# Low-rank products one pair ahead and row work regrouped in the RWKV-7 stage of a decoder step

## The reference

```python
wlog = -softplus(-(w0 + tanh(xw @ w1) @ w2)) - 0.5
decay = exp(-exp(wlog))
a = sigmoid(a0 + (xa @ a1) @ a2)
g = sigmoid(xg @ g1) @ g2
kk = heads(k * p_kk); kk = kk / max(norm(kk), 1e-12)
k = k * (1 + (a - 1) * ka)
S, y = wkv7_scan(S0, r, decay, k, v, -kk, kk * a)
yn = (y - mean(y)) * rsqrt(var(y) + eps) * lnw + lnb
bonus = sum(r * k * rk, -1) * v
out = ((yn + bonus) * g) @ wo
```

## Time and profile before

| what | value |
|---|---|
| three runs | 2943.74, 2944.91 (median), 2949.14 us |
| profiled execution, its own time | 2936.58 us |
| its span | 2934.8 us |
| TensorE, share of the span | 91% |
| VectorE, ScalarE, GpSimd | 56%, 46%, 15% |
| pair stage, from the first key norm sums to the last finish | about 1352 to 1965 us |
| mean granted TensorE clock | 0.963 |

### The profile page before, as it was taken

One profiled execution on the slowest core, in us unless ns is written; L12 is line 12 of the kernel. 1 busy time (PEld: TensorE's weight loads), 2 busy tenths in 40 slices (PEclk: granted clock), 3 DMA queues, 4 the chain that ended last, 5 costly groups with the idle time before them and its releaser, 6 DMA issues.

```text
span 2934.8 us, 69044 instructions
## 1 busy us (share of the span) xinstructions
PE 2683.1 (91%) x25416; PEld 2580.2 (88%) x25416; DVE 1642.7 (56%) x2457; ACT 1352.4 (46%) x2301; POOL 428.3 (15%) x806
## 2 busy tenths in 40 slices
PE   3899999999999699997887778779899999999997
PEld 2799999999999699997666666669899999999997
DVE  7665545654564777335555555634656546654654
ACT  1577435553453455333443444433577435543552
POOL 3221001110112200000111111112112001100112
PEclk7899999999999899999999999989999999999999
DMA  3444444444444444441000000024455444444444
GB/s 114 156 162 152 165 158 157 150 164 157 157 152 144 152 146 168 156 163 69 14 25 25 25 25 25 25 85 165 140 161 168 168 160 163 164 165 165 164 144 142
DMA packets 113726, 378.37 MB, mean 129 GB/s; under 512 B 12080, under 2 KB 22960, under 8 KB 113328
## 3 DMA queue, kind: packets, MB, share of 16 engines
q1 hardware_dynamic: 113584, 376.26, 38.2%
HBM read 363.61 MB, written 12.60 MB: 128 GB/s over the span
## 4 chain that ended last, share of the span: by engine, by line
PE 87%; DVE 7%; ACT 3%; issue 3%; POOL 0%; DMA 0%; DVEq 0%; ACTq 0%; POOLq 0%
PE bank L542 24%; PE bank L544 24%; PE bank L543 24%; PE bank L654 11%; PE bank L620 1%; DVE ysd L1289 1%; DVE pext L1358 1%; ACT L1012 1%; DVE tb L1266 1%; PE bank L794 0%; PE bank L853 0%; DVE ar L1296 0%; PE bank L797 0%; PE bank L604 0%; DVE rnorm L1148 0%
## 5 line engine op out<-in xcount | busy, mean ns | idle before, releaser
L1141 DVE TENSOR_TENSOR wlo<-raw,whi 128x1024 fp32r<-128x1024 f32 (+1 forms) x672 | 794.5, 1197 | 776.7 <-ACT whi L875 775.8
L542 PE MATMUL bank<-h_hi,whi 128*128 128x290 f32 (+1 forms) x3520 | 1059.3, 301 | 45.2 <-DVE h_lo L1167 38.1
L875 ACT ACTIVATE whi<-raw 128x1024 fp32r<-128x1024 f32 (+1 forms) x672 | 685.3, 1032 | 836.5 <-PE bank L544 815.2
L544 PE MATMUL bank<-h_hi,wlo 128*128 128x290 f32 (+1 forms) x3520 | 1056.8, 300 | 0.0
L543 PE MATMUL bank<-h_lo,whi 128*128 128x290 f32 (+1 forms) x3520 | 1056.0, 300 | 0.0
L542 PEld LDWEIGHTS bank<-h_hi,whi 128*128 128x128 f32 x3520 | 668.2, 190 | 49.7 <-issue 44.2
L543 PEld LDWEIGHTS bank<-h_lo,whi 128*128 128x128 f32 x3520 | 668.7, 190 | 0.0
L544 PEld LDWEIGHTS bank<-h_hi,wlo 128*128 128x128 f32 x3520 | 668.5, 190 | 0.0
L542 PE MATMUL bank<-act_hi,whi 128*128 128x304 f32 (+1 forms) x1376 | 410.1, 298 | 1.1 <-DVE act_lo L1226 1.1
L544 PE MATMUL bank<-act_hi,wlo 128*128 128x304 f32 (+1 forms) x1376 | 410.4, 298 | 0.0
L543 PE MATMUL bank<-act_lo,whi 128*128 128x304 f32 (+1 forms) x1376 | 409.7, 298 | 0.0
(11 more groups left out here) (209 smaller groups left out, 3024.9 us busy)
## 6 DMA issues: line engine op xcount, KB each, us to landing
raw<-W_all SPq DMA_DIRECT2D x648, 512.0 KB, 3.3
raw<-W_all SPq DMA_DIRECT2D x32, 192.0 KB, 3.1
wkv_out<-sout SPq DMA_DIRECT2D x16, 288.0 KB, 2.2
l<-L_all SPq DMA_DIRECT2D x16, 256.0 KB, 2.8
s<-wkv_st SPq DMA_DIRECT2D x16, 256.0 KB, 3.0
x<-xT SPq DMA_DIRECT2D x4, 608.0 KB, 6.1
x_spill<-x SPq DMA_DIRECT2D x1, 2432.0 KB, 7.2
x<-x_spill SPq DMA_DIRECT2D x1, 2432.0 KB, 9.4
```

The lines of the kernel that those rows point to most:

```text
L542: mm_(acc, wh, xh, start=first, stop=False)
L544: return mm_(acc, wl, xh, start=False, stop=last)
L875: activation(WHI[q][:, 0:n], RAW[q][:, 0:n], ACT.Copy).then_inc(whi_ready, 1)
L1141: tt(WLO[q][:, 0:n], RAW[q][:, 0:n], WHI[q][:, 0:n].bitcast(f32), ALU.subtract).then_inc(wlo_ready, 1)
```

## The change

The decay's and a's low-rank products of pair n+1 are made in the joint of iteration t, behind the bonus sums, beside the gate products of pair n, which move there from the joint's end. They write to banks 6, 7 and 1. ScalarE's tanh, exp, tanh and KP for pair n+1 follow in the joint, then the gate copy. The mean sums wait for KP (`kp_ready`), since they use bank 7, and the final state products for the gate copy. A new first iteration t = -2 makes the two products for pair 0. ScalarE's `affine` goes from step 0 to step 3, VectorE's `k_rows` from step 4 to step 3. SP loads L2 before it waits for the output state. The copy of y waits for `at_ready` in place of `out_ready` where there is an inverse.

```diff
@@ pipeline
+        iteration(FIRST_STAGE, 0, operands=False, inverse=False, chain=False, finish=False)
         iteration(-1, 1, inverse=False, chain=False, finish=False)
@@ SP, pair_io
-                sp.wait_ge(fin_ready, p)
-                sp.dma_start(wkv_out[p - 1].rearrange("p (b n) -> p b n", b=9), SOUT).then_inc(wkv_stored, 16)
                 if weights:
                     sp.wait_ge(gg_ready, p + 1)
                     sp.dma_start(L2[i], L2_all[p + 2]).then_inc(l2_loaded[i], 16)
+                sp.wait_ge(fin_ready, p)
+                sp.dma_start(wkv_out[p - 1].rearrange("p (b n) -> p b n", b=9), SOUT).then_inc(wkv_stored, 16)
@@ TensorE, steps
                     if operands and s_ == 0:
-                        if later(n):
-                            pe.wait_ge(gg_ready, n)
+                        if chain and later(j):
+                            pe.wait_ge(var_ready, j)
+                        elif not chain:
+                            pe.wait_ge(kp_ready, n + 1)
                         pe.wait_ge(kksq_ready, n + 1)
...
-                    if operands and s_ == 1:
-                        pe.wait_ge(kkroot, n + 1)
-                        pe.wait_ge(l2_loaded[m], by_parity(n, m))
-                        mm_(bank[7][:, 0:TOK], L2[m][:, 0:128], hidden[:, 0, :], start=True, stop=True).then_inc(z_mm, 1)
-                    if operands and s_ == 2:
-                        pe.wait_ge(gates_ready, n + 1)
-                        mm_(bank[7][:, 0:TOK], L2[m][:, 128:256], hidden[:, 1, :], start=True, stop=True).then_inc(lora_mm, 1)
@@ TensorE, joint, behind the bonus sums
+                if gates:
+                    pe.wait_ge(l2_loaded[par], by_parity(n + 1, par))
+                    if operands:
+                        pe.wait_ge(kkroot, n + 1)
+                    wide(bank[6], L2[par], 0, 0).then_inc(z_mm, 1)
+                    wide(bank[7], L2[par], 128, 1).then_inc(lora_mm, 1)
+                if operands:
+                    wide(bank[1], L2[m], 256, 2, stop=False)
+                    wide(bank[1], L2[m], 384, 3, start=False).then_inc(gate_mm, 1)
                 if chain:
-                    pe.wait_ge(*((kp_ready, n + 1) if operands else (gg_ready, PAIRS)))
+                    if gates:
+                        pe.wait_ge(kp_ready, n + 2)
                     pe.wait_ge(y_ready, j + 1)
...
+                    if operands:
+                        pe.wait_ge(gg_ready, n + 1)
                     pe.wait_ge(sax_ready, j + 1)
...
+                    if gates:
+                        pe.wait_ge(gates_ready, n + 2)
                     waited()
                     turned(bank[5], BR)
                     turned(bank[6], KR).then_inc(trans_bk_mm, 1)
-                    pe.wait_ge(*((var_ready, j + 1) if chain else (kp_ready, n + 1)))
-                    mm_(bank[7][:, 0:TOK], L2[m][:, 256:384], hidden[:, 2, :], start=True, stop=False)
-                    mm_(bank[7][:, 0:TOK], L2[m][:, 384:512], hidden[:, 3, :], start=False, stop=True).then_inc(gate_mm, 1)
@@ ScalarE
-                    if finish and s_ == 0:
+                    if finish and s_ == 3:
                         act.wait_ge(scaled, t - 1)
                         activation(YY[par_], YY[par_], ACT.Identity, scale=par("lnw", t - 2), bias=par("lnb", t - 2)).then_inc(affine, 1)
...
-                        if finish:
-                            act.wait_ge(out_ready, t - 1)
+                        act.wait_ge(*((at_ready, t + 1) if inverse else (out_ready, t - 2)))
                         act.wait_ge(y_mm, j + 1)
                         activation(YY[m], bank[0][:, 0:TOK], ACT.Copy).then_inc(y_ready, 1)
+                if gates:
+                    act.wait_ge(z_mm, n + 2)
+                    steps.done(activation(DEC[:, 0:TOK], bank[6][:, 0:TOK], ACT.Tanh, bias=w0_half[:, ds(n + 1)], scale=0.5))
+                    steps.wait()
+                    activation(DEC[:, 0:TOK], DEC[:, 0:TOK], ACT.Exp, scale=0.5 * DECAY_SCALE, bias=decay_bias)\
+                        .then_inc(gates_ready, 1)
+                    act.wait_ge(lora_mm, n + 2)
+                    if operands:
+                        act.wait_ge(rkk_ready, n + 1)
+                    steps.done(activation(TA[:, 0:TOK], bank[7][:, 0:TOK], ACT.Tanh, bias=a0_half[:, ds(n + 1)], scale=0.5))
+                    steps.wait()
+                    activation(KP[:, 0:TOK], TA[:, 0:TOK], ACT.Identity, scale=ka_half[:, ds(n + 1)], bias=ka_rest[:, ds(n + 1)])\
+                        .then_inc(kp_ready, 1)
                 if operands:
+                    act.wait_ge(gate_mm, n + 1)
+                    act.sem_inc(act_gate, 1)
+                    activation(k_all[:, n, :], bank[1][:, 0:TOK], ACT.Copy).then_inc(gg_ready, 1)
                     act.wait_ge(x2_mm, n + 1)
@@ VectorE
-                steps_n = {1: norms, 2: decays, 3: b_rows, 4: k_rows}
+                def rows():
+                    b_rows()
+                    k_rows()
+
+                steps_n = {1: norms, 2: decays, 3: rows}
```

More of the change, by code:

```diff
@@ L303, in build @@
         y_mm s_mm sp_ready s_ready y_ready sax_ready vx_ready fin_mm fin_ready mean_mm centered ycsq_ready gram_b_mm
-        sout_ready stk_ready trans_bk_mm var_mm var_ready gnroot scaled affine out_ready wkv_stored tile_gate pool_gate""".split()
+        sout_ready stk_ready trans_bk_mm var_mm var_ready gnroot scaled affine out_ready wkv_stored tile_gate pool_gate act_gate""".split()
     (lora_mm, gate_mm, kksum_mm, bonus_mm, trans_mm, gram_mm, gates_ready, kp_ready, kksq_ready, kkroot,
@@ L309, in build @@
      sout_ready, stk_ready, trans_bk_mm, var_mm, var_ready, gnroot, scaled, affine, out_ready, wkv_stored,
-     tile_gate, pool_gate) = [sem(n) for n in RSEMS]
+     tile_gate, pool_gate, act_gate) = [sem(n) for n in RSEMS]
     xset_ready = [sem(f"xset_ready{z}") for z in range(2)]
     s0_loaded = [sem(f"s0_loaded{i}") for i in range(2)]
+    FIRST_STAGE = -2
     LV = 5
@@ L668, in iteration @@
                 n, m, j = t + 1, 1 - par, t - 1
+                gates = not isinstance(t, int) or t + 2 < PAIRS
                 def t1_products(l, z):
@@ L821, in iteration @@
                     head_sums(bank[5], TB).then_inc(bonus_mm, 1)
+                wide = lambda dst, l2, at, i, start=True, stop=True: mm_(dst[:, 0:TOK], l2[:, at:at + 128], hidden[:, i, :],
+                                                                       start=start, stop=stop)
+                if gates:
[7 more added lines that the diff above has]
+                    wide(bank[1], L2[m], 384, 3, start=False).then_inc(gate_mm, 1)
                 if chain:
-                    pe.wait_ge(*((kp_ready, n + 1) if operands else (gg_ready, PAIRS)))
+                    if gates:
+                        pe.wait_ge(kp_ready, n + 2)
                     pe.wait_ge(y_ready, j + 1)
@@ L1038, in iteration @@
                 if operands:
-                    act.wait_ge(gate_mm, n + 1)
                     act.wait_ge(trans_bk_mm, n + 1)
@@ L1043, in iteration @@
                     ins.then_inc(tok_act, 1)
-                    activation(k_all[:, n, :], bank[7][:, 0:TOK], ACT.Copy).then_inc(gg_ready, 1)
             decay_bias = 0.5 * DECAY_SCALE
```

## The result

The changed kernel takes 2973.73 us (median of 4 runs, 2973.1 to 2975.51) against 2944.32 us of the kernel before on the same chips (4 runs). The ratio is 1.0098, interval 1.0084 to 1.0112: 1% slower. The sign was forecast, the size was not: +29 us against +6, outside the range of 2932 to 2962.

A forecast was written before the change was run, and what follows sets the result against it. TensorE was taken as the bound, busy 80% at mean clock 0.92 in the loop. Full-clock pairs +2.4, clock +2.0 and ends +1.8 made +6.2 us on 2944.9: 2951.1, range 2932 to 2962.

The forecast's parts named there:

- The joint: Stretch from Gram products to the pair's end: two added products and the mean's wait for ScalarE, +2.1 us a pair.
- The tanh table load is hidden: In the joint: ScalarE stands idle during the Gram products, so the load adds nothing to the mean's wait.
- rival E: In the joint: the tanh load isn't hidden, 13 x 1.28 = +16.6 us, giving 2967.7; chance 0.06.
- The affine's place: Moved from step 0 to step 3: step 0 to 1 gains 1.3 us, AR comes 1.2 later.
- The wait for KP: In the joint, before the mean sums: TensorE idles 0.7 to 0.8 us until ScalarE's KP.
- the steps: Steps 0 to 3, update to update: gains of 1.3, 1.3 and 0.5 us a pair, VectorE's T1 coming last.
- Step 0 to 1: With affine moved, RHS is early and T1 comes last: gain 1.3 us a pair.
- GpSimd's two operations: Step 3 to the joint: they hold up VectorE's tb and AR products, Gram products 1.2 us later; bounds 0 to 1.65.
- moving the rows: Step 3 to the joint: key and bonus rows change places with T1 of step 4, cost 0.
- the back edge: At the loop's end: TensorE's wait keeps its 2.7 us, bounds -1 to +1 in each of five.
- The clock: Half clock in all twelve joints, +8.3 us; less half clock in step 1, -6.3; together +2.0.
- The ends: Before and after the loop: start and first pairs +6.8 us, last iterations and chain -5.0, together +1.8.

The follow-up runs named there:

- e1: The changed kernel with a one-element tanh on ScalarE behind the copy of y, ahead of the wait for the z product: 2947.8 us.
- e3: The changed kernel with the decay tanh's bias taken from one fixed column instead of the loop's: 2944.84 us, one run.
- e2: The changed kernel with ScalarE's affine at the end of step 1 instead of step 3: 2949.59 us.
- e8: The kernel before with only the key rows and the bonus product moved into step 3: 2931.78 us.
- e7: The changed kernel with an early tanh load, the affine at the end of step 1 and the mean sums ahead of the z product: 2917.65 us.
- e4: The kernel before with only ScalarE's affine moved from step 0 to step 3: 2953.36 us.

## Why the prediction was wrong

**The step that failed** is the one in "The joint" that says "The tanh table load is hidden: ScalarE stands idle there during the Gram products, and the sqrt load of the same joint ran before its wait". It was reasoned from a load whose activation has no operand indexed by the loop. That was rival E, put at 0.06 and priced at 1.28 us a pair. e1 and e3 show it, at 26 us with what the clock added; E's own price was 16.6. Without that term the time lies in the range: with the load early the kernel takes 2947.8, 3 us from the forecast 2951.1. The affine's place costs nearly as much (24 us, e2), but that stood in the sum, as 1.2 us a pair and 8.3 by the clock. The wait for KP, forecast at 0.7 to 0.8, is then 0.9.

**Right within the working:** the steps. Clean distances of the kernel after are 4.62 and 4.28 us from update to update (4.6 and 4.4 forecast), and T1 became the last to come. Step 0 to 1: 6.62 to update 1, 6.8 forecast. The steps' gain is 3.6 us a pair, forecast 3.1 and 0.5 by the clock.

**GpSimd's two operations:** Gram products 0.8 us later than before, 1.2 forecast. The two moves inside that number were mixed: the affine in step 3 costs 1.2 (after against e2), and moving the rows gains 0.4 (before against e8), which I had put at 0. So the stall was sized rightly and the rows' own gain was missed: with the rows first, part of SAX falls beside T1 of step 4, and in e8 the first AR product is stretched by 0.6 us where `tb` had lost 0.94.

**The joint** was forecast at +2.1. It came to 4.3 a pair: 2.1, the load's 1.3, 0.6 by half clock behind the longer wait, and the back edge. Its wait, one in every second pair, was 2.4 to 2.8 us and is now 3.2 to 3.6, where I had kept 2.7 with bounds of 1: 0.3 a pair.

**The clock.** All twelve joints now begin at half clock, as forecast: 4.05 us from Gram products to bonus sums against 2.96, 1.1 a pair where I had 0.7 (five more slow joints). The slow ones also became slower, with 4.29 in seven of them, so that the Gram products ran at half clock throughout. In the steps the prediction counted seven pairs with half clock in step 1; the trace of before has five of them (6.7 to 6.9 us from update 1 to 2), worth 4.2 us and not 6.3.

**The ends.** The stage begins its loop 5.0 us later (1435.8 against 1430.8), 6.8 forecast. From the last operands' pair to the last finish 82.9 us against 84.5: 1.6 gained, 5.0 forecast; the joint of that pair too starts at half clock (4.29 us to the bonus sums instead of 2.20), which I had counted at the clean pair's length.

**Together:** 5.0 + 32.1 - 1.6 = 35.5 of the 36.5 us between the two profiled spans. The medians differ by 29.4, since the profiled execution of before lay 8 us under its median. Which of the stretches above are too large by these 7 us isn't known.

**Open:** why the back edge takes longer. It is 2.4 to 2.8 us in the kernel before, 3.2 to 3.6 after, up to 3.9 in e7. No run was made on it. Also open is the move of the products by itself: no run has it without another part of the change.

## What to carry to other kernels

When a ScalarE function is moved to where it starts a chain, its table load counts as part of the chain until the trace shows it ahead of the wait; a one-element activation of the same function with fixed operands, placed ahead of the wait, settles it. Work handed from one engine to another has to be followed to the end: in step 3 the affine held up nothing on ScalarE and cost 1.2 us a pair because GpSimd's two operations behind it then met VectorE's two-operand operations on the way to the next matrices. When several parts are changed at once, try each alone: here one part gained 13 us by itself and two placements lost some 50 between them.

## What the runs showed that I had not expected

- A table load of 1.28 us stood ahead of its activation's wait where the operands were fixed, and behind it where the bias was indexed by the loop's register, because the instruction that works out the address took the wait (e3 against the kernel after).
- In the same place, TensorE kept full clock behind a wait of 0.9 us in all six joints where no back edge follows and fell to half clock behind 2.2 us in four of them, at 1.65 us each (e1 against after).
- Removing an early wait may only move the clock's fall to the next quiet place (e4: half clock left step 1 and came to step 2 and to every joint), and moving the key and bonus rows alone brought ten of twelve joints to full clock, while the steps lost as much again in the profiled execution (e8).
